# Memory attention of a streaming encoder step: prompt scores directly behind the second key product, sample parts in one three-bank result, query weights between key loads

## The chip, the cores and the metric

The kernel runs on one core of one Trainium2 chip. The metric is the device time of one execution in microseconds (us). PE is TensorE, DVE is VectorE, ACT is ScalarE, POOL is GpSimd; SP is the engine from whose queue most transfers are issued.

## The reference, cut to what matters

One layer with three parallel branches for 1024 prompt rows and 8 x 16 sample rows, then a merge and a ConvFFN. The change is in the third branch, cross-attention to 256 memory tokens with 4 heads of width 256. The prompt group computes its memory keys and values here; the sample group reads its own from a cache.

```python
def _mem_kv(mem, g, w):
    kv = (_rmsnorm(mem, g) @ w).reshape(B, M, 2, MEM_HEADS, MEM_DH)
    return (transpose(kv[:, :, 0], (0, 2, 1, 3)), transpose(kv[:, :, 1], (0, 2, 1, 3)))

def _mem_attention(q, mk, mv):
    q = q.reshape(B, L, MEM_HEADS, MEM_DH)
    logits = einsum('blhd,bhmd->bhlm', q, mk) * (MEM_DH ** -0.5)
    p = softmax(logits, axis=-1)
    return einsum('bhlm,bhmd->blhd', p, mv).reshape(B, L, MEM_HEADS * MEM_DH)
```

The prompt's keys and values per head (`new_mem_k_prompt`, `new_mem_v_prompt`) are outputs as well.

## The kernel before, in words

The program is a row of phases. `mem_phase` is the third branch. It runs its four heads one after the other: three in a hardware loop, the fourth written behind it (`head(MH - 1, last=True)`). The engines run apart and meet at semaphores. Each engine executes its own list in the order in which it is written.

**Results.** PE writes into two groups of four PSUM banks (512 float32 each), in turn. `Results` lists what a head writes, in order: K0, SL, K1, PTS, KR, S, V, OS, PT, OT, O0, O1, X, Y. `take` makes PE wait until the result two places back has been read (`free`); `ready` makes a reader wait until the result is whole (`full`); `freed` marks it as read.

One head on PE (`head` in the tensor block, lines 1741 to 1847):
- K0, K1 (`memory_keys`): the two halves of the head's memory keys, in split precision, 24 matmuls each. SL between them: the sample group's scores (L1765). ACT copies K0 and K1 to `mem_kt` (L1601). DVE and ACT make the softmax of SL (L1689, L1690, L1597, L1695 to L1697).
- PTS: four transposes of the sample probabilities (L1774); ACT copies them to `sample_probs_t` (L1604). KR: four transposes of the keys for the output (L1781); ACT copies them (L1607) and stores them (L1609).
- S: the prompt's scores, 16 products in two recorded passes (L1787). DVE takes the row maximum (L1689) and subtracts it (L1690), ACT takes the exponential (L1614), DVE sums (L1695), inverts (L1696) and scales (L1697). This last step releases PT.
- V: the memory values (L1800 to L1802). ACT copies them to `mem_v_rows` (L1616).
- OS: the sample's output (L1811), copied by ACT (L1623). PT: 16 transposes of the prompt's probabilities (L1818), copied by ACT (L1625). OT: four transposes of OS (L1824).
- O0, O1: the prompt's output (L1836). X, Y and "riders" in spare banks of OT, O0, O1: the next head's queries (L165 to L167), in six pieces. The first piece is in OT and needs the query weights W_Q[0]; the first that needs W_Q[1] is in X.

**Weights.** Blocks of 128 x 1024 go through two slots: SP loads one (`load_w`, L107) once POOL has finished the block before it in that slot, ACT rounds it to `weight_hi` (`round_w`, L113), POOL subtracts to get `weight_lo` (`rest_w`, L118), PE takes both (`w_parts`). A head uses six: W_K (2, from the head before), W_V (2), W_Q (2). In the fourth head, the W_Q slots take the next phase's branch weights.

**SP's order in a head** (`head`, lines 1537 to 1548): W_V[0], W_V[1]; the 32 loads of the next head's cached keys (`load_k`, L1530, eight streams with four loads each); W_Q[0], W_Q[1]; the next head's W_K; the eight loads of the next cached values (L1535). In the fourth head, there are no key or value loads. The cached keys are turned by DVE (L1679), streams 0 to 3 after PT, streams 4 to 7 after O1.

**ACT's order in a head**, behind K1: round W_V[1]; copy PTS; copy and store KR; exponential of S; copy V; round W_Q[0] and W_Q[1]; store the values; copy OS; copy PT.

Of the kernel before, what the change touches and what calls it, by code (L numbers as in the profile page):

```python
# [10 lines left out]
ACT = mybir.ActivationFunctionType  # L11
AX = mybir.AxisListType
ds = bass.ds

P = 128
D = 1024
KT = D // P
SEQ, DEC_B, DEC_S, PAST = 1024, 8, 16, 1024
ROWS = SEQ + DEC_B * DEC_S
NT = ROWS // P  # L20
PT = SEQ // P
# [3 lines left out]
MEM, MH, MD = 256, 4, 256  # L25
# [364 lines left out]
def flat(ap):  # L390
    return ap.rearrange("p a n -> p (a n)")
# [1075 lines left out]
def mem_phase(g):  # L1467
# [7 lines left out]
    MT = MEM // P  # L1475
    mq, yc = (g.sb(n, [P, 2, ROWS], ctx=ctx) for n in ("mem_q", "mem_out"))
    mk, mkr, mvr, ps_s, pt_s, qp = (g.sb(n, [P, 2, 256], ctx=ctx) for n in (
        "mem_kt", "mem_k_rows", "mem_v_rows", "sample_probs", "sample_probs_t", "mem_query_blocks"))
# [5 lines left out]
    gcol = g.sb("mem_norm_col", [P, KT], ctx=ctx)  # L1484
    rows, tmp = pr[:].rearrange("p (t a) n -> p t (a n)", t=MT), flat(pt[:]).rearrange("p (k n) -> p k n", k=KT)
    consts_in, cb = g.consts, g.cb
    kt_r = g.sem("cached_mem_k_turned")
    kc_in = [g.sem(f"cached_mem_k{n}_in") for n in range(2)]
    vc_in, sq_r, root_r, scaled, mhi_r, mlo_r, zero_r, qp_r = (g.sem(n) for n in (
        "cached_mem_v_in", "mem_squares", "mem_root", "mem_scaled",  # L1490
# [1 line left out]
    shift_r, probs_r, s_shift_r, s_probs_r, out_mk, out_mv, out_y = (g.sem(n) for n in (  # L1492
        "mem_shifted", "mem_probs_ready", "mem_sample_shifted", "mem_sample_probs_ready", "mem_k_out", "mem_v_out",
        "y2_out"))
    NW = 6
    first = 2
    W_K, W_V, W_Q = (first, first + 1), (first + 2, first + 3), (first + 4, first + 5)
    pre = Results(g, ["Q0", "N", "Q1"])
    g.r += pre.n
    loop_R = Results(g, ["K0", "SL", "K1", "PTS", "KR", "S", "V", "OS", "PT", "OT", "O0", "O1", "X", "Y"])  # L1500
    last_R = Results(g, [n for n in loop_R.k if n not in ("X", "Y")])
    last_R.base += (MH - 1) * loop_R.n
    assert loop_R.n % 2 == 0 and last_R.n % 2 == 0
# [6 lines left out]
    with nc.Block() as block:  # L1510
        @block.sync
        def _(sp):
            sp.dma_start(rows, g.x["mem_prompt"][0].rearrange("(t p) d -> p t d", p=P)).then_inc(consts_in, 16)
            with nc.allow_non_contiguous_dma(reason="columns of 1024 values"):
                sp.dma_start(gcol[:], columns(g.x["mem_norm"][0])).then_inc(consts_in, 16)

            def wkv(v, n, i):

                w = g.x["w_mem_kv"][0].rearrange("(k p) n -> p k n", p=P)
                return w[:, :, ds(i * MD + (v * D + n * P), P)]  # L1520

            def wq(n, i):
                return g.w_in(W_MQ + n, i, 2)

            def load_k(i):

                for b in range(DEC_B):
                    blocks = g.x["cache_mem_k"][0, b, ds(i, 1)].rearrange("h (r j) (c n) -> r (h j c) n", r=BLOCK, c=2)
                    for q in range(P // BLOCK):
                        sp.dma_start(kc[q * BLOCK:(q + 1) * BLOCK, b].rearrange("r c (j n) -> r (c j) n", n=BLOCK),  # L1530
                                     blocks[:, :, q * BLOCK:(q + 1) * BLOCK]).then_inc(kc_in[b // 4], 16)

            def load_v(i):
                for b in range(DEC_B):
                    sp.dma_start(vc[:, b], g.x["cache_mem_v"][0, b, ds(i, 1)].rearrange("h (t p) d -> p (h t) d", p=P))\  # L1535
                        .then_inc(vc_in, 16)

            def head(i, following, last=False):
                for n in range(2):
                    g.load_w(sp, wkv(1, n, i), W_V[n], i, NW)  # L1540
                if not last:
                    sp.wait_ge(kt_r, i * 2 + 2)
                    load_k(i + 1)
                for j, view in enumerate(following):
                    g.load_w(sp, view, W_Q[0] + j, i, NW)
                if not last:
                    sp.wait_ge(g.full, loop_R.full_value("OS", i))
                    load_v(i + 1)
            g.load_w(sp, wkv(0, 0, 0), W_K[0])
            g.load_w(sp, wkv(0, 1, 0), W_K[1])  # L1550
            load_k(0)
            load_v(0)
            with sp.Fori(0, MH - 1) as i:
                head(i, (wq(2, i), wq(3, i), wkv(0, 0, i + 1), wkv(0, 1, i + 1)))
            wb = g.x["w_branch"][0, 0].rearrange("(k p) n -> p k n", p=P)

            head(MH - 1, (wb[:, :, 0:P], wb[:, :, P:2 * P]), last=True)

        @block.scalar
        def _(act):  # L1560
            ps = pre.ready(act, "Q0")
# [10 lines left out]
            ps = pre.ready(act, "Q1")  # L1572
# [9 lines left out]
            def head(i, last=False):  # L1582
                R, r = (last_R, 0) if last else (loop_R, i)
# [4 lines left out]
                def finish(n, ins):  # L1588

                    if n in riders and not last:  # L1590
                        ins = query(*riders[n], g.psum[(R.base + R.k[n]) % 2], 3)
                    R.freed(ins, n)
                for n in range(2):
                    if n == 1:
                        ps = R.ready(act, "SL", r)
# [4 lines left out]
                    ps = R.ready(act, f"K{n}", r)  # L1600
                    finish(f"K{n}", act.activation(mk[:, n, :], ps[:, 0, 0:MEM], ACT.Copy))  # L1601
                    g.round_w(act, W_V[n], i, NW)
                ps = R.ready(act, "PTS", r)
                finish("PTS", act.activation(flat(pt_s[:]), ps[:, 0, :], ACT.Copy))  # L1604
                act.wait_ge(out_mk, i * 16 + 16)
                ps = R.ready(act, "KR", r)
                finish("KR", act.activation(mkr[:], ps[:, 0, :].rearrange("p (t n) -> p t n", t=MT), ACT.Copy))  # L1607
                R.wait_freed(act, "KR", r)
                act.dma_start(g.o["mk_prompt"][0, 0, ds(i, 1)].rearrange("h (t p) d -> p (h t) d", p=P), mkr[:])\  # L1609
                    .then_inc(out_mk, 16)  # L1610
                act.wait_ge(out_mv, i * 16 + 16)
                act.wait_ge(shift_r, i + 1)
                ps = R.ready(act, "S", r)
                finish("S", act.activation(flat(pr[:]), flat(ps), ACT.Exp))  # L1614
                ps = R.ready(act, "V", r)
                finish("V", act.activation(mvr[:], ps[:, 0, :].rearrange("p (t n) -> p t n", t=MT), ACT.Copy))  # L1616
                for n in range(2):
                    g.round_w(act, W_Q[n], i, NW)
                R.wait_freed(act, "V", r)
                act.dma_start(g.o["mv_prompt"][0, 0, ds(i, 1)].rearrange("h (t p) d -> p (h t) d", p=P), mvr[:])\  # L1620
                    .then_inc(out_mv, 16)
                ps = R.ready(act, "OS", r)
                finish("OS", act.activation(ps_s[:], ps[:, 0:2, 0:MD], ACT.Copy))  # L1623
                ps = R.ready(act, "PT", r)
                finish("PT", act.activation(flat(pt[:]), flat(ps), ACT.Copy))  # L1625
                act.wait_ge(out_y, i * 16 + 16)
                ps = R.ready(act, "OT", r)
# [3 lines left out]
                for c in range(2):  # L1631
                    ps = R.ready(act, f"O{c}", r)
# [3 lines left out]
                if not last:  # L1636
                    g.round_w(act, W_K[0] + NW, i, NW)
                    ps = R.ready(act, "X", r)
# [86 lines left out]
        def _(pe):  # L1725
# [15 lines left out]
            def head(i, last=False):  # L1741
# [5 lines left out]
                def take(n):  # L1747

                    ps = R.take(pe, n, r)
                    if n in riders and not last:  # L1750
                        return ps, query(ps, 3, *riders[n])
                    return ps, None
# [14 lines left out]
                                            start=(c == 0), stop=(c == 1))  # L1767
                ins.then_inc(g.full, 1)
                memory_keys(1)
                ps, _ = take("PTS")  # L1770
                pe.wait_ge(s_probs_r, i + 1)
                for n in range(2):
                    for m in range(MT):
                        ins = pe.transpose(ps[:, 0, (n * MT + m) * P:(n * MT + m + 1) * P],  # L1774
                                           ps_s[:, n, m * P:(m + 1) * P], g.ident[:])
                ins.then_inc(g.full, 1)
                ps, _ = take("KR")
                R.wait_freed(pe, "K1", r)
                for t in range(MT):
                    for n in range(2):  # L1780
                        ins = pe.transpose(ps[:, 0, t * MD + n * P:t * MD + (n + 1) * P], mk[:, n, t * P:(t + 1) * P],  # L1781
                                            g.ident[:])
                ins.then_inc(g.full, 1)
                ps, _ = take("S")
                for t in range(PT):
                    for n in range(2):
                        ins = pe.matmul(ps[:, t // 2, (t % 2) * MEM:(t % 2 + 1) * MEM], mq[:, n, t * P:(t + 1) * P],  # L1787
# [1 line left out]
                ins.then_inc(g.full, 1)  # L1789

                ps, _ = take("V")
                for n in range(2):
                    g.w_parts(pe, W_V[n], i, NW)
                wh, wl = (t[:].rearrange("p n (k c) -> p k n c", c=P) for t in (g.whi, g.wlo))
                if (g.w + W_V[0]) % 2:
                    raise ValueError("the first value block stands in the first slot")
                for t in range(MT):
                    rows_t, o = slice(t * P, (t + 1) * P), ps[:, 0, t * MD:(t + 1) * MD].rearrange("p (n c) -> p n c", c=P)
                    for k in range(KT):
                        pe.matmul(o, mhi[:, k, rows_t], wh[:, k], start=(k == 0), stop=False)  # L1800
                        pe.matmul(o, mlo[:, k, rows_t], wh[:, k], start=False, stop=False)
                        ins = pe.matmul(o, mhi[:, k, rows_t], wl[:, k], start=False, stop=(k == KT - 1))  # L1802
                ins.then_inc(g.full, 1)
                ps, _ = take("OS")
                R.wait_freed(pe, "PTS", r)
                pe.wait_ge(vc_in, i * 128 + 128)
                pv = flat(pt_s[:]).rearrange("p (n m q) -> p n m q", n=2, m=MT)
                for n in range(2):
# [870 lines left out]
```

## Time and profile before

| what | us |
|---|---|
| median of 3 runs | 3334.06 (3327.71 to 3336.87) |
| profiled execution, its own time | 3333.16 |
| its span in the profile | 3331.4 |
| PE busy, whole span | 3145.9 (94%) |
| DVE, ACT, POOL busy | 1388.3, 1127.7, 874.1 |
| the four heads, K0 of the first to the merge's first matmul | 1726.85 to 2004.63 |

A row of the timeline gives the start and the duration in us, the engine, the line, what is written and read, a count, and in brackets how long the engine was idle before it and what released it. A row of waits gives who waited for whom: total, times, longest. Where two rows of one engine overlap, that is its pipeline.

### The profile page before, as it was taken

To read this page: it belongs to the slowest core of one execution; us is meant where nothing else is said; L and a number is where in the kernel's file an instruction comes from. 1 tells how busy PE (TensorE), PEld (TensorE's weight loads), DVE (VectorE), ACT (ScalarE), POOL (GpSimd) and SP (SyncE) were. 2 spreads that over 40 slices of the span, in tenths; PEclk is the share of its full clock that TensorE was granted. 3 is DMA by queue.
4 is the path that set the end of the run, shared out by engine and by line. 5 is a ranking of instruction groups with operands and counts; after the bars stand their busy time and mean duration, and the time that the engine had idled before them with its cause. 6 is when DMAs were issued, how large, how long until landed. Compare 5 with 4: busy or idle time off the path is not lost. (4 is left out here: it accounts for less than half of the span.)

```text
span 3331.4 us, 50040 instructions
## 1 busy us (share of the span) xinstructions
PE 3145.9 (94%) x19550; PEld 2959.6 (89%) x19550; DVE 1388.3 (42%) x1446; ACT 1127.7 (34%) x1586; POOL 874.1 (26%) x520
## 2 busy tenths in 40 slices
PE   6999999999999999999679889999979999999997
PEld 5999999999988888888467769999979999999996
DVE  5554444544344555455522212222044444444433
ACT  3344433444234444444432221122242222222222
POOL 2433233332211121121011211343342322322220
PEclk8999999999999999999789899999989999999998
DMA  5212121112157787678665526432211111111101
GB/s 158 72 46 66 56 69 55 50 60 63 57 112 152 153 138 121 139 147 142 120 144 127 134 91 208 148 105 67 79 51 45 44 38 44 39 42 38 38 25 68
DMA packets 684752, 295.69 MB, mean 89 GB/s; under 512 B 350524, under 2 KB 665436, under 8 KB 684680
## 3 DMA queue, kind: packets, MB, share of 16 engines
q1 hardware_dynamic: 680232, 285.90, 35.2%
q10 hardware_dynamic: 4448, 8.80, 0.7%
q8 instruction: 49, 0.80, 0.1%
q14 instruction: 23, 0.19, 0.0%
HBM read 240.23 MB, written 54.41 MB: 88 GB/s over the span
## 5 line engine op out<-in xcount | busy, mean ns | idle before, releaser
L118 POOL TENSOR_TENSOR weight_lo<-weight_stage,weight_hi 128x1024 fp32r<-128x1024 f32 x180 | 452.4, 2515 | 1483.3 <-ACT weight_hi L113 1483.3
L1862 PE MATMUL group<-act_hi_part,weight_hi 128*128 128x384 f32 x1056 | 360.8, 342 | 13.6 <-DVE act_lo_part L2091 9.3
L1863 PE MATMUL group<-act_lo_part,weight_hi 128*128 128x384 f32 x1056 | 359.8, 341 | 0.0
L1864 PE MATMUL group<-act_hi_part,weight_lo 128*128 128x384 f32 x1056 | 359.7, 341 | 0.0
L165 PE MATMUL group<-h_hi_part,weight_hi 128*128 128x384 f32 x936 | 331.5, 354 | 9.9 <-POOL weight_lo L118 4.8
L113 ACT ACTIVATE weight_hi<-weight_stage 128x1024 fp32r<-128x1024 f32 x180 | 190.7, 1061 | 419.8 <-PE group L2133 231.6
L166 PE MATMUL group<-h_lo_part,weight_hi 128*128 128x384 f32 x936 | 317.2, 339 | 0.0
L167 PE MATMUL group<-h_hi_part,weight_lo 128*128 128x384 f32 x936 | 317.0, 339 | 0.0
L2131 PE MATMUL group<-act_hi_part,weight_hi 128*128 128x384 f32 x768 | 259.5, 338 | 11.9 <-DVE act_lo_part L2044 11.9
L2132 PE MATMUL group<-act_lo_part,weight_hi 128*128 128x384 f32 x768 | 258.6, 337 | 0.0
L2133 PE MATMUL group<-act_hi_part,weight_lo 128*128 128x384 f32 x768 | 258.6, 337 | 0.0
L1350 PE MATMUL group<-h_hi_part,weight_hi 128*128 128x384 f32 x696 | 243.8, 350 | 1.1 <-ACT next_v L1096 1.0
L1350 PE MATMUL group<-h_hi_part,weight_lo 128*128 128x384 f32 x696 | 237.8, 342 | 0.0
L1350 PE MATMUL group<-h_lo_part,weight_hi 128*128 128x384 f32 x696 | 235.6, 339 | 0.0
L1862 PEld LDWEIGHTS group<-act_hi_part,weight_hi 128*128 128x128 f32 x1056 | 199.6, 189 | 17.1 <-issue 9.9
L698 DVE COPY_PREDICATED scores<-level_masks,group 128x1152 f32<-128x1152 uint32 (+2 forms) x88 | 92.2, 1078 | 285.1 <-PE group L823 283.9
L1863 PEld LDWEIGHTS group<-act_lo_part,weight_hi 128*128 128x128 f32 x1056 | 199.7, 189 | 0.0
L1864 PEld LDWEIGHTS group<-act_hi_part,weight_lo 128*128 128x128 f32 x1056 | 199.6, 189 | 0.0
L165 PEld LDWEIGHTS group<-h_hi_part,weight_hi 128*128 128x128 f32 x936 | 178.5, 191 | 16.5 <-POOL weight_lo L118 5.1
L166 PEld LDWEIGHTS group<-h_lo_part,weight_hi 128*128 128x128 f32 x936 | 178.3, 191 | 4.3 <-issue 3.3
L167 PEld LDWEIGHTS group<-h_hi_part,weight_lo 128*128 128x128 f32 x936 | 177.9, 190 | 0.0
L2408 DVE TENSOR_TENSOR residual<-residual,group 128x1152 f32<-128x1152 f32 x80 | 108.3, 1354 | 163.3 <-PE group L2523 163.3
(348 smaller groups left out, 6694.3 us busy)
## 6 DMA issues: line engine op xcount, KB each, us to landing
weight_stage<-in_w_in SPq DMA_DIRECT2D x88, 512.0 KB, 4.8
cached_v<-in_cache_diff_v SPq DMA_DIRECT2D x128, 256.0 KB, 5.0
cached_k<-in_cache_diff_k SPq DMA_DIRECT2D x224, 128.0 KB, 4.2
weight_stage<-in_w_up SPq DMA_DIRECT2D x44, 512.0 KB, 3.8
y_stage<-scratch_y_branch SPq DMA_DIRECT2D x24, 576.0 KB, 9.4
gate_in<-scratch_gates SPq DMA_DIRECT2D x24, 576.0 KB, 3.7
weight_stage<-in_w_branch SPq DMA_DIRECT2D x24, 512.0 KB, 3.9
down_stage<-in_w_down SPq DMA_DIRECT2D x22, 512.0 KB, 3.6
```

The costliest lines, as they stand in the source:

```text
L113: act.activation(self.whi[:, n % 2, :], self.wst[:, n % 2, :], ACT.Copy).then_inc(self.w_hi, 1)
L118: pool.tensor_tensor(self.wlo[:, n % 2, :], self.wst[:, n % 2, :], self.whi[:, n % 2, :].bitcast(F32), ALU.subtract).then_inc(self.w_lo, 1)
L165: pe.matmul(out, wh[:, k, :], xh[:, k, cols], start=(k == 0), stop=False)
L166: pe.matmul(out, wh[:, k, :], xl[:, k, cols], start=False, stop=False)
L167: last = pe.matmul(out, wl[:, k, :], xh[:, k, cols], start=False, stop=(k == KT - 1))
L1350: ins = pe.matmul(rider_bank, w[:, k, :], x[:, k, c * CW:(c + 1) * CW], start=(at == 0), stop=(at == STEPS - 1))
L1862: pe.matmul(o, w[0][:, k, :], ahi[:, k, rows], start=(k == 0), stop=False)
L1863: pe.matmul(o, w[0][:, k, :], alo[:, k, rows], start=False, stop=False)
L1864: last = pe.matmul(o, w[1][:, k, :], ahi[:, k, rows], start=False, stop=(k == KT - 1))
L2131: pe.matmul(o, wh[:, k, :], ahi[:, k, cols], start=(k == 0 and open_sum), stop=False)
L2132: pe.matmul(o, wh[:, k, :], alo[:, k, cols], start=False, stop=False)
L2133: last = pe.matmul(o, wl[:, k, :], ahi[:, k, cols], start=False, stop=(k == KT - 1))
```

## The change

Three things, all in `mem_phase`.

1. PE computes S directly behind K1. The transposes of sample probabilities and keys go behind it.
2. PTS and KR are no results of their own any more. Both are written into banks 0 and 1 of V's group, the values into bank 2. A head has 12 results instead of 14. ACT reads the three in a row once V is whole: sample probabilities, keys, values. A new semaphore, `turned_r`, tells PE that the sample probabilities are copied; OS waits for it. The key store is issued beside the value store.
3. SP issues W_Q[0] behind the key loads of streams 0 to 2, and W_Q[1] behind those of stream 3, instead of both behind all eight. ACT rounds W_Q[1] behind the copy of OS instead of ahead of it.

```diff
-    loop_R = Results(g, ["K0", "SL", "K1", "PTS", "KR", "S", "V", "OS", "PT", "OT", "O0", "O1", "X", "Y"])
+    loop_R = Results(g, ["K0", "SL", "K1", "S", "V", "OS", "PT", "OT", "O0", "O1", "X", "Y"])
...
-                    load_k(i + 1)
-                for j, view in enumerate(following):
-                    g.load_w(sp, view, W_Q[0] + j, i, NW)
+                    load_k(i + 1, range(0, 3))
+                g.load_w(sp, following[0], W_Q[0], i, NW)
+                if not last:
+                    load_k(i + 1, range(3, 4))
+                g.load_w(sp, following[1], W_Q[1], i, NW)
+                if not last:
+                    load_k(i + 1, range(4, DEC_B))
+                for j, view in enumerate(following[2:]):
+                    g.load_w(sp, view, W_Q[1] + 1 + j, i, NW)
...
-                ps = R.ready(act, "PTS", r)
-                finish("PTS", act.activation(flat(pt_s[:]), ps[:, 0, :], ACT.Copy))
-                act.wait_ge(out_mk, i * 16 + 16)
-                ps = R.ready(act, "KR", r)
-                finish("KR", act.activation(mkr[:], ps[:, 0, :].rearrange("p (t n) -> p t n", t=MT), ACT.Copy))
-                R.wait_freed(act, "KR", r)
-                act.dma_start(g.o["mk_prompt"][0, 0, ds(i, 1)].rearrange("h (t p) d -> p (h t) d", p=P), mkr[:])\
-                    .then_inc(out_mk, 16)
-                act.wait_ge(out_mv, i * 16 + 16)
                 act.wait_ge(shift_r, i + 1)
                 ps = R.ready(act, "S", r)
                 finish("S", act.activation(flat(pr[:]), flat(ps), ACT.Exp))
                 ps = R.ready(act, "V", r)
-                finish("V", act.activation(mvr[:], ps[:, 0, :].rearrange("p (t n) -> p t n", t=MT), ACT.Copy))
-                for n in range(2):
-                    g.round_w(act, W_Q[n], i, NW)
+                act.activation(flat(pt_s[:]), ps[:, 0, :], ACT.Copy).then_inc(turned_r, 1)
+                act.wait_ge(out_mk, i * 16 + 16)
+                act.wait_ge(out_mv, i * 16 + 16)
+                act.activation(mkr[:], ps[:, 1, :].rearrange("p (t n) -> p t n", t=MT), ACT.Copy)
+                finish("V", act.activation(mvr[:], ps[:, 2, :].rearrange("p (t n) -> p t n", t=MT), ACT.Copy))
+                g.round_w(act, W_Q[0], i, NW)
                 R.wait_freed(act, "V", r)
+                act.dma_start(g.o["mk_prompt"][0, 0, ds(i, 1)].rearrange("h (t p) d -> p (h t) d", p=P), mkr[:])\
+                    .then_inc(out_mk, 16)
...
                 finish("OS", act.activation(ps_s[:], ps[:, 0:2, 0:MD], ACT.Copy))
+                g.round_w(act, W_Q[1], i, NW)
...
-                R.wait_freed(pe, "PTS", r)
+                pe.wait_ge(turned_r, i + 1)
```

On PE, the place is the head from the last matmul of K1 (L152) to the first of V. Before:

```order
L152 MATMUL group<-mem_hi_part,weight_lo 128x256
L370 REGISTER_ALU
L1774 MATMUL group<-ident,sample_probs 128x128 x4
L1781 MATMUL group<-ident,mem_kt 128x128 x4
L370 REGISTER_ALU
L1787 MATMUL group<-mem_kt,mem_q 128x256 x16
L123 REGISTER_ALU x2
L1800 MATMUL group<-weight_hi,mem_hi_part 128x256
```

And with the change, where the same instructions stand on other lines (L1777 is the scores, L1785 and L1789 the transposes):

```order
L152 MATMUL group<-mem_hi_part,weight_lo 128x256
L370 REGISTER_ALU
L1777 MATMUL group<-mem_kt,mem_q 128x256 x16
L1785 MATMUL group<-ident,sample_probs 128x128 x4
L1789 MATMUL group<-ident,mem_kt 128x128 x4
L123 REGISTER_ALU x2
L1799 MATMUL group<-weight_hi,mem_hi_part 128x256
```

The eight transposes went from ahead of the scores to behind them.

On ACT, the place is the fourth head from the copy of K1 to the copy of PT (in the loop the order is the same). Before:

```order
L1601 ACTIVATE mem_kt<-group 128x256
L113 ACTIVATE weight_hi<-weight_stage 128x1024
L1604 ACTIVATE sample_probs_t<-group 128x512
L1607 ACTIVATE mem_k_rows<-group 128x512
L1609 DMA out_mk_prompt<-mem_k_rows 128x2x256
L1614 ACTIVATE mem_probs<-group 128x2048
L1616 ACTIVATE mem_v_rows<-group 128x512
L113 ACTIVATE weight_hi<-weight_stage 128x1024 x2
L1620 DMA out_mv_prompt<-mem_v_rows 128x2x256
L1623 ACTIVATE sample_probs<-group 128x512
L1625 ACTIVATE mem_probs_t<-group 128x2048
```

And with the change:

```order
L1607 ACTIVATE mem_kt<-group 128x256
L113 ACTIVATE weight_hi<-weight_stage 128x1024
L1611 ACTIVATE mem_probs<-group 128x2048
L1613 ACTIVATE sample_probs_t<-group 128x512
L1616 ACTIVATE mem_k_rows<-group 128x512
L1617 ACTIVATE mem_v_rows<-group 128x512
L113 ACTIVATE weight_hi<-weight_stage 128x1024
L1620 DMA out_mk_prompt<-mem_k_rows 128x2x256
L1622 DMA out_mv_prompt<-mem_v_rows 128x2x256
L1625 ACTIVATE sample_probs<-group 128x512
L113 ACTIVATE weight_hi<-weight_stage 128x1024
L1628 ACTIVATE mem_probs_t<-group 128x2048
```

Two copies went behind the exponential, and one rounding went behind the copy of OS.

On SP, the place is the loop's end of the key loads before the change:

```order
L1530 DMA cached_mem_k<-in_cache_mem_k 32x16x32
L106 REGISTER_ALU
L107 ISA
L107 DMA weight_stage<-in_w_in 128x8x128
L106 REGISTER_ALU
L107 ISA
L107 DMA weight_stage<-in_w_in 128x8x128
L106 REGISTER_ALU
L107 ISA
L107 DMA weight_stage<-in_w_mem_kv 128x8x128
```

And with the change, behind the twelfth of the 32 key loads:

```order
L1530 DMA cached_mem_k<-in_cache_mem_k 32x16x32
L106 REGISTER_ALU
L107 ISA
L107 DMA weight_stage<-in_w_in 128x8x128
L1530 ISA
L1530 DMA cached_mem_k<-in_cache_mem_k 32x16x32
```

The first query block now passes 20 key loads, the second 16.

## Rows read from the trace of the kernel before

**Rows 1.** The page, busy us (share of the span) xinstructions of each engine.

```profile
PE 3145.9 (94%) x19550; PEld 2959.6 (89%) x19550; DVE 1388.3 (42%) x1446; ACT 1127.7 (34%) x1586; POOL 874.1 (26%) x520
```

**Rows 2.** Waits, 1720 to 2000 us: who <- for whom: total, times, longest.

```profile
PE group L1818 <- DVE mem_probs L1697: 13.1, 4, 4.2
...
PE group L1824 <- ACT sample_probs L1623: 8.1, 2, 4.6
```

**Rows 3.** Timeline of head 1 on PE, K1's end to OT.

```profile
1813.76 0.63 PE L1774 MATMUL group<-ident,sample_probs 128*128 128x128 f32 x4 [1.49 <-DVE sample_probs L1697]
1814.23 0.60 PE L1781 MATMUL group<-ident,mem_kt 128*128 128x128 f32 x4
1815.08 7.17 PE L1787 MATMUL group<-mem_kt,mem_q 128*128 128x256 f32 x32 [0.25 <-ACT sample_probs_t L1604]
...
1829.09 1.93 PE L1811 MATMUL group<-cached_mem_v,sample_probs_t 128*32 128x256 f32 x32 [1.09 <-ACT mem_probs L1614]
1833.99 3.46 PE L1818 MATMUL group<-ident,mem_probs 128*128 128x128 f32 x16 [2.97 <-DVE mem_probs L1697]
1840.95 1.09 PE L1824 MATMUL group<-ident,sample_probs 128*128 128x128 f32 x4 [3.50 <-ACT sample_probs L1623]
```

**Rows 4.** Timeline of head 1 on DVE, POOL and ACT.

```profile
1831.55 2.29 DVE L1697 TENSOR_TENSOR mem_probs<-mem_probs,mem_row_sum 128x2048 f32<-128x2048 f32 x1
...
1808.85 2.39 POOL L118 TENSOR_TENSOR weight_lo<-weight_stage,weight_hi 128x1024 fp32r<-128x1024 f32 x1 [0.35 <-ACT weight_hi L113]
...
1812.31 0.38 ACT L1601 ACTIVATE mem_kt<-group 128x256 f32<-128x256 f32 x1 [0.34 <-PE group L152]
...
1827.08 1.88 ACT L1614 ACTIVATE mem_probs<-group 128x2048 f32<-128x2048 f32 x1 [11.57 <-DVE group L1690]
1828.85 0.59 ACT L1616 ACTIVATE mem_v_rows<-group 128x512 f32<-128x512 f32 x1
1837.60 1.06 ACT L113 ACTIVATE weight_hi<-weight_stage 128x1024 fp32r<-128x1024 f32 x1 [8.16 <-DMA weight_stage<-in_w_in]
```

**Rows 5.** Timeline of SP's queue in head 1: issues, and the time they took SP.

```profile
1809.33 23.91 SPq L1530 DMA_DIRECT2D cached_mem_k<-in_cache_mem_k  x32
1833.49 1.03 SPq L107 DMA_DIRECT2D weight_stage<-in_w_in  x2
```

**Rows 6.** Heads 0, 2, 3 on PE and ACT: K1's copy, scores, V's last matmul, OT.

```profile
1743.64 0.42 ACT L1601 ACTIVATE mem_kt<-group 128x256 f32<-128x256 f32 x1
...
1747.76 9.15 PE L1787 MATMUL group<-mem_kt,mem_q 128*128 128x256 f32 x32
...
1885.35 7.17 PE L1787 MATMUL group<-mem_kt,mem_q 128*128 128x256 f32 x32 [0.25 <-ACT sample_probs_t L1604]
...
1897.99 0.28 PE L1802 MATMUL group<-weight_lo,mem_hi_part 128*128 128x256 f32 x1
...
1911.44 1.08 PE L1824 MATMUL group<-ident,sample_probs 128*128 128x128 f32 x4 [4.62 <-ACT sample_probs L1623]
...
1953.62 0.38 ACT L1601 ACTIVATE mem_kt<-group 128x256 f32<-128x256 f32 x1 [0.29 <-PE group L152]
...
1956.70 8.80 PE L1787 MATMUL group<-mem_kt,mem_q 128*128 128x256 f32 x32 [0.51 <-ACT sample_probs_t L1604]
```

**Rows 7.** Timeline of head 3 on POOL and DVE: weight rests beside the scaling.

```profile
1973.62 6.71 POOL L118 TENSOR_TENSOR weight_lo<-weight_stage,weight_hi 128x1024 fp32r<-128x1024 f32 x2 [15.05 <-ACT weight_hi L113]
...
1974.71 3.42 DVE L1697 TENSOR_TENSOR mem_probs<-mem_probs,mem_row_sum 128x2048 f32<-128x2048 f32 x1
```

**Rows 8.** Windows, head 2: us, PE, PEld, DVE, ACT, POOL busy (x), PEclk, DMA share, GB/s.

```profile
1904.20:1911.40 7.20, 2.56 (x16) 2.19 (x16) 2.31 (x1) 2.70 (x4) 2.10 (x1) 0.58 0.66 182
```

**Rows 9.** Timeline of PE, head 2: query matmuls behind OT.

```profile
1912.18 0.67 PE L165 MATMUL group<-h_hi_part,weight_hi 128*128 128x384 f32 x1
...
1915.94 0.34 PE L165 MATMUL group<-h_hi_part,weight_hi 128*128 128x384 f32 x1
1916.11 0.34 PE L166 MATMUL group<-h_lo_part,weight_hi 128*128 128x384 f32 x1
```

More of the change, by code:

```diff
@@ L1486, in mem_phase @@
     consts_in, cb = g.consts, g.cb
-    kt_r = g.sem("cached_mem_k_turned")
+    kt_r, turned_r = g.sem("cached_mem_k_turned"), g.sem("sample_probs_turned")
     kc_in = [g.sem(f"cached_mem_k{n}_in") for n in range(2)]
@@ L1523, in wq, with load_k @@
                 return g.w_in(W_MQ + n, i, 2)
-            def load_k(i):
-                for b in range(DEC_B):
+            def load_k(i, streams):
+                for b in streams:
                     blocks = g.x["cache_mem_k"][0, b, ds(i, 1)].rearrange("h (r j) (c n) -> r (h j c) n", r=BLOCK, c=2)
@@ L1550, in _ @@
             g.load_w(sp, wkv(0, 1, 0), W_K[1])
-            load_k(0)
+            load_k(0, range(DEC_B))
             load_v(0)
@@ L1769, in head @@
                 memory_keys(1)
[L1770 to L1777, printed above, removed]
-                R.wait_freed(pe, "K1", r)
[L1779 to L1784, printed above, removed]
+                ps, _ = take("S")
+                R.wait_freed(pe, "K1", r)
                 for t in range(PT):
@@ L1791, in head @@
                 ps, _ = take("V")
+                pe.wait_ge(s_probs_r, i + 1)
+                for n in range(2):
+                    for m in range(MT):
+                        pe.transpose(ps[:, 0, (n * MT + m) * P:(n * MT + m + 1) * P],
+                                           ps_s[:, n, m * P:(m + 1) * P], g.ident[:])
+                for t in range(MT):
+                    for n in range(2):
+                        pe.transpose(ps[:, 1, t * MD + n * P:t * MD + (n + 1) * P], mk[:, n, t * P:(t + 1) * P],
+                                            g.ident[:])
                 for n in range(2):
@@ L1797, in head @@
                 for t in range(MT):
-                    rows_t, o = slice(t * P, (t + 1) * P), ps[:, 0, t * MD:(t + 1) * MD].rearrange("p (n c) -> p n c", c=P)
+                    rows_t, o = slice(t * P, (t + 1) * P), ps[:, 2, t * MD:(t + 1) * MD].rearrange("p (n c) -> p n c", c=P)
                     for k in range(KT):
```

## The prediction

> **What bounds the kernel now.** I read the page first: PE is busy for 94% of the span [rows 1], so little can be won outside PE's gaps. Then the waits in the stretch of the memory heads: PE stands 13.1 us before PT (L1818) for DVE's scaling, in all four heads, and 8.1 us before OT (L1824) for ACT's copy of OS, in two [rows 2]. Then the timeline of head 1. The reader is to see two chains.
>
> The first begins at the scores S: they start at 1815.08, and PT, which needs their softmax, at 1833.99 [rows 3]. These 18.91 us are S on PE, two passes of DVE, the exponential on ACT (from 1827.08), the sum, the inverse and the scaling on DVE (1831.55 + 2.29 = 1833.84) [rows 4]. PE's own work between (V, OS) is shorter: it stands 1.09 and 2.97 us [rows 3]. So PT moves with the start of S, us for us, as long as V and OS still fit in. S itself waits for what stands ahead of it: the sample transposes, which wait 1.49 us for the sample softmax [rows 3].
>
> The second is the weights. ACT can't copy OS before it has rounded both query blocks, and it stands 8.16 us for the first, until 1837.60 [rows 4]. The block was late at its issue: SP issued 32 key loads from 1809.33 for 23.91 us and the query blocks only at 1833.49 [rows 5]. OT starts at 1840.95 after 3.50 us of idle PE [rows 3], in head 2 after 4.62 [rows 6]; and the waits name no third head [rows 2].
>
> The heads are a serial chain on PE, and the phases behind them too, so what is won in a head should stay won.
>
> **The change, part by part.**
>
> *S directly behind K1.* S now waits for ACT's copy of K1 alone. In head 1 that ends at 1812.31 + 0.38 = 1812.69 [rows 4]; with 0.1 for the semaphore S starts at 1812.8 instead of 1815.08: **2.3 us**. Head 2 repeats head 1: **2.3**. In head 0 the copy ends at 1744.06, S started at 1747.76: **3.6**. In head 3 it ends at 1954.00, S started at 1956.70: **2.6** [rows 6]. The chain from S to PT is unchanged, so PT comes earlier by the same.
>
> *Do the moved parts still fit?* Counted from the start of S: V's last matmul ended at 1897.99 + 0.28 - 1885.35 = 12.9 us [rows 6]. The eight transposes now stand ahead of V; four took 0.47 from start to start [rows 3], so eight add 0.95, and V is whole at 13.9. The exponential ends at 1827.08 + 1.88 - 1815.08 = 13.9 too. Then ACT copies the sample probabilities, and OS can start at about 14.6, instead of 14.0; it takes 1.93 [rows 3] and ends at 16.6. PT starts at 18.9. So OS is later and PE still waits there, 2.3 us: nothing is lost. Two results less cost nothing, their waits went with them. The key store's issue goes from before the exponential to beside the value store; both stand ahead of the copy of OS on ACT's queue. That copy isn't late until PT has ended, 21.5 at the earliest, against 16.6 + 0.6: cover of 4 us.
>
> *Query weights earlier.* A key load costs SP 23.91 / 32 = 0.75 us. W_Q[0] goes out behind 12 of them, at 1809.33 + 9.0 = 1818.3 (its slot is free: the rest of W_V[0] was done at 1808.85 + 2.39 = 1811.24 [rows 4]). Before, it was rounded 1837.60 - 1833.49 = 4.1 us behind its issue; now it lands at some 1822.5, and ACT wants it only at 1828.2. If the loads around it doubled its time it were still in time. W_Q[1] follows at 1821.8, lands at 1826, is wanted at 1830. Key loads of streams 3 to 7 come 0.5 to 1 us later, DVE turns stream 3 behind PT, 10 us after its landing, and the others behind O1: covered. So the wait before OT goes: **3.5 us** in head 1, **4.6** in head 2. What is late next there is PT itself, whose end releases OT.
>
> *The scaling and POOL.* In head 3 the scaling (L1697) took 3.42 us instead of 2.29, while POOL worked on weight rests that had started 1.09 before it; the two rests took 6.71, against 2.39 for one elsewhere [rows 4, 7]. One reading fits both to the tenth: POOL's first rest ran alone until about 1975.9, then DVE's 2.29 until 1978.13, then the second rest until 1980.3. That is no slower work, but one waiting for the whole of the other. The Trainium skill ("SBUF — State Buffer", section "Who interferes with whom") says so: a DVE instruction with two SBUF inputs and a GpSimd instruction that reads SBUF exclude each other, and whichever issues first holds the port for its whole length. By that rule the trace agrees, and the rule speaks against this change.
>
> For the change moves a rest to exactly this place in all four heads. From S's start: pt_s copied from 13.9, keys and values at intervals of 0.48 (a copy's busy 0.59, overlapped), W_Q[0] rounded from 15.4 to 16.4 (1.06 us [rows 4]), POOL at 16.5. The scaling starts at 1831.55 - 1815.08 = 16.47. That is a tie within what these numbers can tell. Bounds: if DVE is first, 0, and head 3 gets back its 3.42 - 2.29 = **1.1 us**; if POOL is first, the scaling waits up to 2.4, PT comes 2.3 us later in each head. I take DVE first: each of my shortcuts (a switch between kinds of matmul, ACT's additional waits for the stores) makes POOL later, none makes DVE later.
>
> *PE's clock.* After the long wait for OT the granted clock was down: 0.58 over the stretch from PT to OT in head 2 [rows 8], that is in good part the lower level, 1.2 of 2.4 GHz. The query matmuls then went 12 in 3.76 us, where 12 take 2.1 at 0.17 [rows 9]: 1.7 lost. Head 3's scores took 8.80 instead of 7.17 [rows 3, 6]: 1.6 lost after the gaps around the transposes, and these gaps go. Bounds: 0, and 1.7 + 1.6 with at most another 1.7 in head 1 = 5.0. PE still has gaps before OS and PT, and PT may lose in head 2 what the query wins, so I take **2**.
>
> *Sum.* 3.6 + (2.3 + 3.5) + (2.3 + 4.6) + (2.6 + 1.1) = 20.0, and 2 for the clock: 22 us. The profiled execution took 3333.16 of its own time, 0.9 under the median of the runs. 3333.16 - 22 = **3311 us**.
>
> **Rivals.**
>
> *POOL gets the port first.* Then the scaling waits 2.3 us in each head, and the gain of S directly behind K1 is used up: 4 x 2.3 = 9.3 less. 3311 + 9 = 3320. For it: the tie; a mere 0.1 us decides. Against it: it needs V to be whole no later than 13.9 in every head. By the skill's rule and this order it would be this time.
>
> *PE's clock recovers everywhere, in head 0's scores (9.15 against 7.17) as well.* Upper bound 5.0 + 2.0 instead of 2: 3306. For it: shorter gaps in all heads; against it: PE stands some 3 us before head 0's scores as before.
>
> *The query blocks come late from between the key loads (slower).* Place: ACT's rounding of W_Q[1], which now stands ahead of the copy of PT. If the small loads around it hold it up, the copy, O0, O1 and all behind wait. Before, the copy of PT began behind OT's start at 1840.9; for a head to lose, W_Q[1] must land after 1839.9 (1.06 us of rounding ahead of that), 18 us behind its issue at 1821.8, instead of 4.1. At 25 us the copy of PT would begin 7 us later than before in three heads, and head 3 would keep its gain: 3333 + 21 - 4 = 3350. Against it: measured landings; nothing in the trace comes near.
>
> *The change does not take effect:* S isn't earlier because K1's copy is itself held up on ACT by a weight (in head 0 it stood behind one). Only the weights' gain stays, 8.1 + 1.1: 3324.
>
> **How the numbers follow.** About 0.3%, 10 us, is what a measurement of this kernel can tell from no change; the runs shown lie within 9 us. Chances: the forecast 0.55, POOL first (in most heads) 0.30, full clock 0.08, no effect 0.04, late blocks 0.03. The range goes from 3303 (full clock, and a few us of spread between runs) to 3323 (POOL first with no clock won back: 3322). Under 3324 is faster: the forecast, the full clock, and most of POOL first: 0.88. Within 10 us: the rest of it and no effect: 0.10. Slower: 0.02.
>
> **What would show it.** In the trace after: in heads 1 and 2 S within 0.2 us behind K1's copy; no idle before OT; PT 18.9 us behind the start of S at full clock. If the scaling takes 4 to 4.7 us with a POOL rest started just before it, POOL was first. If it takes 2.29 and POOL's rest 4 to 4.7, DVE was. If ACT stands before a rounding of W_Q for a load, the place between the key loads is too late. I am wrong if PT doesn't move with S, or if the heads get shorter and the phases behind them longer.

## The result and the profile after

The changed kernel takes 3297.26 us (median of 4 runs, 3292.19 to 3301.82) against 3332.64 for the kernel before on the same chip (4 runs): ratio 0.9896, 95% interval 0.9883 to 0.9909. That is 35 us faster, 30 to 39 by the interval. I had forecast 3311 with a range of 3303 to 3323: the direction was right, the gain was half as large again, and the range misses it. The profiled execution is the longest of the four, 3301.82; it is 31.3 us under the profile before, and it misses the range too. What follows explains these 31.3; no profile was taken of a run near 3292, so some 4 us of the median's gain stay without a place.

First the page of the changed kernel; the line answers to [rows 1].

```profile
PE 3131.9 (95%) x19550; PEld 2949.7 (89%) x19550; DVE 1387.6 (42%) x1446; ACT 1128.4 (34%) x1586; POOL 881.0 (27%) x520
```

PE has the same 19550 matmuls and is busy for 14 us less. So it isn't only waits that went. To see where, I cut both traces at the same events: K0 of head 0, the end of the copy of K1 in each head, the merge's first matmul. Windows of the kernel before (us, PE, PEld, DVE, ACT, POOL busy, PEclk, DMA share, GB/s), first the stretch ahead of the heads, the heads together, and the stretch behind them; then heads 0 to 3, each from its copy of K1 to the next:

```profile
0.00:1726.85 1726.85, 1633.55 (x10809) 1489.54 (x10809) 841.40 (x1079) 707.95 (x1066) 421.29 (x224) 0.98 0.46 100
1726.85:2004.63 277.78, 225.84 (x1377) 192.20 (x1377) 70.31 (x50) 77.56 (x97) 56.79 (x23) 0.90 0.48 128
2004.63:3331.40 1326.77, 1286.56 (x7366) 1277.87 (x7366) 476.64 (x319) 342.23 (x424) 396.03 (x274) 0.98 0.21 66
...
1744.06:1812.69 68.63, 62.23 (x380) 54.24 (x380) 17.78 (x13) 20.61 (x26) 15.89 (x7) 0.93 0.51 131
1812.69:1882.96 70.27, 60.97 (x380) 53.50 (x380) 16.93 (x12) 20.41 (x27) 14.19 (x6) 0.95 0.51 129
1882.96:1954.00 71.04, 60.62 (x380) 52.98 (x380) 16.88 (x13) 19.13 (x26) 14.19 (x6) 0.93 0.49 126
1954.00:2004.63 50.63, 30.80 (x157) 22.63 (x157) 12.76 (x10) 13.29 (x14) 9.05 (x3) 0.80 0.26 90
```

And of the changed kernel:

```profile
0.00:1726.55 1726.55, 1632.37 (x10808) 1489.23 (x10809) 841.74 (x1079) 708.62 (x1066) 421.83 (x224) 0.97 0.46 100
1726.55:1973.03 246.48, 212.76 (x1376) 182.35 (x1377) 69.31 (x50) 77.50 (x97) 63.05 (x23) 0.96 0.55 144
1973.03:3300.00 1326.97, 1286.80 (x7366) 1278.11 (x7366) 476.57 (x319) 342.30 (x424) 396.11 (x274) 0.98 0.21 66
...
1743.66:1808.34 64.68, 60.99 (x380) 53.41 (x380) 17.80 (x13) 20.43 (x27) 17.92 (x7) 0.95 0.55 139
1808.34:1869.70 61.36, 57.67 (x380) 50.60 (x380) 16.93 (x13) 20.44 (x27) 16.38 (x6) 1.00 0.59 148
1869.70:1931.05 61.35, 57.67 (x380) 50.60 (x380) 16.87 (x13) 19.14 (x26) 16.37 (x6) 1.00 0.58 146
1931.05:1973.03 41.98, 25.19 (x156) 19.00 (x157) 11.76 (x10) 13.53 (x15) 9.07 (x3) 0.92 0.31 110
```

Ahead of and behind the heads nothing changed. The heads lost 31.3 us (277.78 to 246.48). PE's idle time there, stretch less busy, fell from 51.94 to 33.72: **18.2 us**. Its busy time for the same matmuls fell by **13.1 us**, and the granted clock rose from 0.90 to 0.96, in heads 1 and 2 to 1.00. By heads 0 to 3, idle fell by 2.7, 5.6, 6.7 and 3.0, busy by 1.2, 3.3, 3.0 and 5.6.

The timeline of head 1 on PE in the changed kernel, to be laid beside [rows 3]:

```profile
1808.49 7.14 PE L1777 MATMUL group<-mem_kt,mem_q 128*128 128x256 f32 x32 [0.56 <-ACT mem_kt L1607]
1823.13 1.93 PE L1810 MATMUL group<-cached_mem_v,sample_probs_t 128*32 128x256 f32 x32 [0.87 <-ACT sample_probs_t L1613]
1827.32 1.94 PE L1817 MATMUL group<-ident,mem_probs 128*128 128x128 f32 x16 [2.25 <-DVE mem_probs L1700]
```

S starts 0.15 us behind the copy of K1 (1807.96 + 0.38), PT 18.83 behind S, and there is no gap before OT. PT takes 1.94 where it took 3.46. The groups by line and form in the heads give the sums over all four: S, O and PT, first of the kernel before and then of the changed one (busy, mean ns | idle before).

```profile
L1787 PE MATMUL group<-mem_kt,mem_q 128*128 128x256 f32 x128 | 32.3, 416 | 1.0 <-ACT sample_probs_t L1604 1.0
L1836 PE MATMUL group<-mem_probs_t,mem_v_rows 128*128 128x512 f32 x64 | 30.3, 621 | 1.2 <-ACT mem_probs_t L1625 1.2
L1818 PE MATMUL group<-ident,mem_probs 128*128 128x128 f32 x64 | 13.1, 392 | 13.1 <-DVE mem_probs L1697 13.1
```

```profile
L1777 PE MATMUL group<-mem_kt,mem_q 128*128 128x256 f32 x128 | 30.3, 397 | 4.9 <-ACT mem_kt L1607 4.9
L1835 PE MATMUL group<-mem_probs_t,mem_v_rows 128*128 128x512 f32 x64 | 28.7, 593 | 1.6 <-ACT mem_probs_t L1628 1.6
L1817 PE MATMUL group<-ident,mem_probs 128*128 128x128 f32 x64 | 9.1, 304 | 9.0 <-DVE mem_probs L1700 9.0
```

In head 0 PT still went slowly, behind the same gap as in the other heads:

```profile
1764.33 3.29 PE L1817 MATMUL group<-ident,mem_probs 128*128 128x128 f32 x16 [2.23 <-DVE mem_probs L1700]
```

The other engines in head 1: DVE's scaling, POOL's two rests and ACT's rounding of W_Q[0].

```profile
1824.89 2.29 DVE L1700 TENSOR_TENSOR mem_probs<-mem_probs,mem_row_sum 128x2048 f32<-128x2048 f32 x1
...
1824.90 6.86 POOL L118 TENSOR_TENSOR weight_lo<-weight_stage,weight_hi 128x1024 fp32r<-128x1024 f32 x2 [12.68 <-ACT weight_hi L113]
...
1823.75 1.07 ACT L113 ACTIVATE weight_hi<-weight_stage 128x1024 fp32r<-128x1024 f32 x1
```

The scaling took 2.29, the two rests 6.86; in heads 0 to 2 of the kernel before they took 4.67 to 4.73:

```profile
1838.74 4.67 POOL L118 TENSOR_TENSOR weight_lo<-weight_stage,weight_hi 128x1024 fp32r<-128x1024 f32 x2 [22.18 <-ACT weight_hi L113]
```

DVE was first, by 0.01 us as recorded, and by 0.01 to 0.09 in the other heads. ACT didn't wait for W_Q[0]: no idle is recorded before the rounding.

### The profile page after: what moved, and what is told of

Same layout as the page of the kernel before. It is cut to its first block and busy times, and to the rows that moved or that the text cites. A ratio compares the mean times of both kernels' runs of the same rounds, so it can differ in the third digit from the quotient of the medians.

```text
span 3300.0 us, 50028 instructions
## 1 busy us (share of the span) xinstructions
PE 3131.9 (95%) x19550; PEld 2949.7 (89%) x19550; DVE 1387.6 (42%) x1446; ACT 1128.4 (34%) x1586; POOL 881.0 (27%) x520
## 5 line engine op out<-in xcount | busy, mean ns | idle before, releaser
L118 POOL TENSOR_TENSOR weight_lo<-weight_stage,weight_hi 128x1024 fp32r<-128x1024 f32 x180 | 459.6, 2554 | 1447.1 <-ACT weight_hi L113 1447.0
```

The lines of the kernel that those rows point to most:

```text
L118: pool.tensor_tensor(self.wlo[:, n % 2, :], self.wst[:, n % 2, :], self.whi[:, n % 2, :].bitcast(F32), ALU.subtract).then_inc(self.w_lo, 1)
```

## The experiments

Two theories for the 9 us beyond the forecast's 22: **the clock** (PE's shorter gaps keep the granted clock up, and the same matmuls take less time) and **the waits** (more waits went than I counted). A third question is what each part is worth alone, a fourth the port. The heads' stretch below runs from K0 of head 0 to the merge's first matmul, as above.

**Scores first, weights where they were.** SP's order of the kernel before in the changed kernel. ACT still rounds W_Q[1] behind the copy of OS, so this is the first two parts and ACT's half of the third:

```diff
-                    load_k(i + 1, range(0, 3))
-                g.load_w(sp, following[0], W_Q[0], i, NW)
...
+                    load_k(i + 1, range(DEC_B))
+                for j, view in enumerate(following):
+                    g.load_w(sp, view, W_Q[0] + j, i, NW)
```

> The change without its third part: scores behind K1 and the three-bank result stay, the query weights go out behind all 32 key loads again. Theory (two separate waits, and the clock follows the gaps): in heads 1 and 2 PT starts 2.3 us earlier, but OT still waits for the copy of OS behind the late W_Q[0], and only 1.6 us are won there; head 0 wins 2.2, head 3 (no key loads) its whole 8.6. Sum 14, about 0.4%: some 3319 against 3333. Rival (all of the extra gain comes from the merged results and fewer waits on PE, not from gaps and clock): heads 1 and 2 keep most of their 9 us, 3305 or less.

3325.43 against 3332.61, ratio 0.9979 (0.9968 to 0.999); the stretch 274.01, 3.8 less than before. The sign was right and the size wrong. OT now waits in all three heads of the loop (total idle at the right):

```profile
L1817 PE MATMUL group<-ident,sample_probs 128*128 128x128 f32 x16 | 3.9, 389 | 16.7 <-ACT sample_probs L1619 16.7
...
1837.61 1.09 PE L1817 MATMUL group<-ident,sample_probs 128*128 128x128 f32 x4 [6.04 <-ACT sample_probs L1619]
1839.19 0.69 PE L165 MATMUL group<-h_hi_part,weight_hi 128*128 128x384 f32 x1 [0.49 <-POOL weight_lo L118]
```

What S wins, OT waits longer, for the weights arrive when they did. I had counted 2.2 for head 0, where OT did not wait before: it now waits 4.29. Behind the longer gap the query runs slow for longer: in head 1 about 5.6 us where it was about 2.3. Heads 0 to 2 got longer by 3.6, 1.1 and 0.6 us, head 3 shorter by 8.7. So the first two parts pay in head 3 alone, which has no key loads.

**Weights alone.** The third part on the kernel before (SP as in the diff of the change; on ACT):

```diff
-                for n in range(2):
-                    g.round_w(act, W_Q[n], i, NW)
+                g.round_w(act, W_Q[0], i, NW)
...
                 finish("OS", act.activation(ps_s[:], ps[:, 0:2, 0:MD], ACT.Copy))
+                g.round_w(act, W_Q[1], i, NW)
```

> Only the third part on the kernel before: W_Q[0] behind 12 key loads, W_Q[1] behind 16, ACT rounds W_Q[1] behind the copy of OS. Theory with the port (whichever of DVE's scaling and POOL's rest starts first holds the other off for its whole length): without the three copies ACT rounds W_Q[0] one us earlier, POOL starts 15.4 us behind the scores' start, ahead of the scaling at 16.5; the scaling takes some 3.5 us instead of 2.29 in all four heads and PT is 1.2 later. OT's waits of 3.5 and 4.6 us go, the clock gives 1 to 2: sum 5 to 7, some 3327. Rival (no exclusion, the rows of head 3 were something else): scaling 2.29, sum 9 to 11, 3323.

3322.92, ratio 0.9963 (0.9949 to 0.9977); the stretch 270.71, 7.1 less. The median is the rival's 3323, the 7.1 stands at the upper end of the theory's 5 to 7, so the times do not decide; the rows do. The groups of the scaling and of PT:

```profile
L1703 DVE TENSOR_TENSOR mem_probs<-mem_probs,mem_row_sum 128x2048 f32<-128x2048 f32 x4 | 13.7, 3418 | 0.1
...
L1824 PE MATMUL group<-ident,mem_probs 128*128 128x128 f32 x64 | 14.4, 419 | 16.4 <-DVE mem_probs L1703 16.4
```

The scaling takes 3.42 in all four heads: POOL is first everywhere, as the theory with the port says. PE's gap before PT grew to 4.1, and PT went at the lower clock in all heads (14.4 us against 9.1 in the changed kernel).

So these two kernels give 3.8 and 7.1 us of the stretch, and the whole change 31.3. Each alone runs into a wait that the other part removes or shortens.

**PT delayed.** One more pass on DVE in the changed kernel:

```diff
-                    dve.tensor_tensor(p, p, sm[:, 0:blocks].unsqueeze(2).to_broadcast([P, blocks, MEM]), ALU.mult)\
-                        .then_inc(ready, 1)
+                    ins = dve.tensor_tensor(p, p, sm[:, 0:blocks].unsqueeze(2).to_broadcast([P, blocks, MEM]), ALU.mult)
+                    if blocks == PT:
+                        g.dve.done(ins)
+                        ins = dve.tensor_reduce(sm[:, 0:blocks], p, AX.X, ALU.add)
+                    ins.then_inc(ready, 1)
```

> The change with one more DVE pass (a sum over the scaled probabilities, 2.3 us) between the scaling and its signal to PE, so PE's gap before PT is 4.6 us instead of 2.25 in all four heads. Theory (the extra gain over the forecast is PE's clock, which stays up while the gaps are short): 4 x 2.4 = 9.6 us of delay and besides the transposes of PT at half clock (1.94 becomes 3.5) and the matmuls behind them slow for a while, 2.5 to 4 per head: 18 to 24 us slower than the change, some 3318. Rival (waits alone): 9.6 slower, 3307, with PT still taking 1.94.

3313.69, ratio 0.9939 (0.9922 to 0.9955). The stretch, and PT's group:

```profile
1723.90:1985.22 261.32, 218.08 (x1376) 187.64 (x1377) 78.36 (x53) 77.29 (x97) 62.98 (x23) 0.93 0.52 136
...
L1820 PE MATMUL group<-ident,mem_probs 128*128 128x128 f32 x64 | 13.9, 409 | 18.4 <-DVE mem_row_sum L1703 18.4
```

14.8 more than the changed kernel: idle 43.2 instead of 33.7, which is the delay (18.4 - 9.0 = 9.4 before PT), and 5.3 more of busy PE for the same matmuls. The waits' 9.6 are too few, and my 18 to 24 too many: PT fell to the lower clock in all heads (4.8 of the 5.3), the matmuls behind it hardly did.

**Gaps filled.** Matmuls nobody reads, in the kernel before; no wait is touched:

```diff
+                def fill(o, n):
+                    for k in range(n):
+                        pe.matmul(o, mhi[:, k % KT, 0:P], mhi[:, k % KT, :], start=True, stop=True)
...
+                fill(ps[:, 0, 0:MEM], 18)
                 pe.wait_ge(probs_r, i + 1)
...
+                fill(g.psum[(R.base + R.k["OS"]) % 2][:, 3, 0:MEM], 16)
                 ps = R.take(pe, "OT", r)
```

> The kernel before, with matmuls on the memory parts whose results nobody reads: 18 (2.1 us) in the gap before PT and 16 (1.9 us) behind PT, ahead of OT's wait. No wait is shortened. Theory (clock): PT takes 1.94 instead of 2.56 to 3.65 in all heads, the queries behind OT run at full clock in heads 1 and 2, the products O of head 3 too: 9 to 10 won, 1.9 lost in head 0 where OT has no gap: 7 to 8 us faster than before, 3325. Rival (clock doesn't matter): 0 to 4 us slower than before.

3328.44, ratio 0.9982 (0.9972 to 0.9992): 136 more matmuls make the kernel 3 to 9 us faster (the heads 4.2 shorter in the profile). PT of head 1, and its group:

```profile
1835.94 1.97 PE L1824 MATMUL group<-ident,mem_probs 128*128 128x128 f32 x16 [0.54 <-DVE mem_probs L1697]
...
L1824 PE MATMUL group<-ident,mem_probs 128*128 128x128 f32 x64 | 9.3, 308 | 3.4 <-DVE mem_probs L1697 3.4
```

PT took 1.97 in heads 0 to 2 and still 3.44 in head 3; this, a longer gap ahead of the sample transposes in head 0 (5.81 us against 5.06) and the scores of head 2 (8.86 us against 7.17) kept the gain under the 7 to 8 expected. PT still starts 18.83 us behind S in head 1 (18.91 before), so no wait got shorter. That the time of equal matmuls falls when PE's gaps are filled, with every wait in place, is shown for PT in heads 0 to 2.

**The changed kernel again**, beside the next three on another chip.

> The changed kernel again, on the same chip as the three below. Theory: the stretch of the heads takes 246 to 247 us as before, with 212 to 213 us of busy PE in it; if the time differs from the first profile's 3302, the difference lies in other phases. Rival (the heads themselves come out differently from run to run, by the clock): the stretch differs by over 3 us.

3301.05 against 3331.8, ratio 0.9903 (0.9886 to 0.992). Its stretch:

```profile
1727.46:1974.25 246.79, 212.42 (x1376) 182.15 (x1377) 69.19 (x49) 76.79 (x96) 62.95 (x23) 0.96 0.55 143
```

The heads repeat to 0.3 us; the 3.0 us between the two profiles lie ahead of them (0.9) and behind them (1.8). But where PE goes slowly does not repeat: here head 0's PT took 1.94, and head 2's, which took 1.94 in the first profile, went slowly behind the same gap:

```profile
1888.53 3.52 PE L1817 MATMUL group<-ident,mem_probs 128*128 128x128 f32 x16 [2.25 <-DVE mem_probs L1700]
```

**No common result.** Scores first and the weights' new places, but PTS and KR stay results of their own, behind S:

```diff
-"K1", "PTS", "KR", "S", "V", "OS"
+"K1", "S", "PTS", "KR", "V", "OS"
```

> Scores directly behind K1 and the weights' new places, but the sample transposes and the key transposes stay results of their own, each in the whole group, behind the scores (K1, S, PTS, KR, V). Theory (two groups in turn: KR must wait until the exponential has read S, 13.9 us behind the start of S): V starts at 14.6 instead of 7.8, OS ends at 22.7, PT starts at 22.8 instead of 18.9: 3.9 us per head and PE's clock low in V behind a gap of 6: 16 to 26 us slower than the change, 3313 to 3323. Rival (merging the three only saves a few semaphore waits): within 4 us of the change.

3322.05, ratio 0.9965 (0.9952 to 0.9977). KR in head 1, and the stretch:

```profile
1825.18 1.11 PE L1793 MATMUL group<-ident,mem_kt 128*128 128x128 f32 x4 [6.27 <-ACT mem_probs L1611]
...
1725.34:1990.96 265.62, 218.40 (x1376) 187.16 (x1377) 69.30 (x50) 77.55 (x96) 54.52 (x23) 0.91 0.51 134
```

18.8 us more than the change. KR waits 6.27 for the exponential, since it needs S's group, and V with it. Against the weights alone (270.71) the new place of S brings only 5.1 us of the stretch here: most of its worth hangs on the three banks.

**The port.** W_Q[0] rounded ahead of the copies of keys and values:

```diff
                 act.activation(flat(pt_s[:]), ps[:, 0, :], ACT.Copy).then_inc(turned_r, 1)
+                g.round_w(act, W_Q[0], i, NW)
...
-                g.round_w(act, W_Q[0], i, NW)
```

> The change with one thing moved on ACT: W_Q[0] is rounded directly behind the copy of the sample probabilities, ahead of the copies of keys and values, so that POOL's rest starts one us earlier, 15.5 us behind the start of S instead of 16.5. Theory (the port goes to whichever starts first, for its whole length): the scaling's 2.29 becomes 3.4 to 3.7 in all four heads, PT comes 1.2 later, its gap grows to 3.4 and its clock falls in some heads: 5 to 11 us slower than the change. Rival (no exclusion, or no tie): scaling 2.29, no difference over 2 us, since nothing else waits for those copies.

3313.22, ratio 0.9947 (0.993 to 0.9964): 12 us more than the change on the same chip by the medians. Head 1, and the stretch:

```profile
1825.98 3.55 DVE L1700 TENSOR_TENSOR mem_probs<-mem_probs,mem_row_sum 128x2048 f32<-128x2048 f32 x1
...
1825.02 2.36 POOL L118 TENSOR_TENSOR weight_lo<-weight_stage,weight_hi 128x1024 fp32r<-128x1024 f32 x1 [11.66 <-ACT weight_hi L113]
...
1829.68 1.94 PE L1817 MATMUL group<-ident,mem_probs 128*128 128x128 f32 x16 [3.51 <-DVE mem_probs L1700]
...
1724.63:1981.98 257.35, 217.99 (x1377) 186.91 (x1377) 74.30 (x49) 77.24 (x97) 57.16 (x23) 0.93 0.53 138
```

POOL's rest ends at 1827.38; the scaling, issued at 1825.98, ends 2.15 us after that: it waited for nearly all of what was left of the rest, as "Who interferes with whom" in "SBUF — State Buffer" of the Trainium skill says. That is 1.26 us in heads 1 and 2 (1.25 and 1.34 in the others), and 10.6 in the stretch: 5.0 of idle, 5.6 of busy PE. In head 1 PT took 1.94 all the same; in the other heads it took 2.75 to 3.65.

**Softmax in halves.** DVE's work on the first four row blocks runs while PE makes the other four:

```diff
+                    if t == PT // 2 - 1:
+                        ins.then_inc(half_r, 1)
...
+                for h in range(2):
+                    if h == 0:
+                        dve.wait_ge(half_r, i + 1)
+                    else:
+                        R.ready(dve, "S", r)
+                    v, m = s[:, h * H:(h + 1) * H], mx[:, h * H:(h + 1) * H]
+                    g.dve.done(dve.tensor_reduce(m, v, AX.X, ALU.max))
+                    dve.tensor_tensor(v, v, m.unsqueeze(2).to_broadcast([P, H, MEM]), ALU.subtract).then_inc(shift_r, 1)
```

> The change with the prompt softmax in two halves of four row blocks: DVE's maximum and subtraction of the first half run while PE still makes the second, the exponential and the scaling go by halves, PT by halves. Theory (PE's gap before PT is the chain S, DVE, ACT, DVE): the scaling ends at some 15.5 us behind the start of S instead of 18.8, PT follows OS with no gap: 4 x 2.25 = 9 us less idle, 1 to 2 of clock in head 0: 9 to 11 us faster than the change, ratio to before 0.986. Rival (the rest of POOL, now without the scaling beside it, or the copy of OS becomes what OT waits for): 4 us or less.

3290.38, ratio 0.9869 (0.9852 to 0.9885), where the change on the same chip had 0.9903. The stretch, and the scaling of head 1 as two instructions:

```profile
1725.08:1963.22 238.14, 212.49 (x1376) 181.64 (x1377) 70.77 (x61) 77.52 (x100) 54.39 (x23) 0.95 0.58 149
...
1818.46 2.36 DVE L1722 TENSOR_TENSOR mem_probs<-mem_probs,mem_row_sum 128x1024 f32<-128x1024 f32 x2
```

8.7 us less than the change, all of it idle (25.7 against 34.4); the busy time is the same, so the 1 to 2 us of clock that I expected did not come: head 0's scores took 9.93 us where they took 8.53. S started at 1805.06, so the scaling ends 15.8 behind it, and PT has no gap. This kernel beats the changed one, by 10.7 us by the medians.

## Why the prediction was wrong, step by step

- *S directly behind K1* and *the parts still fit*: right. In head 1, 18.83 from S to PT where I had 18.91, OS at 14.64 behind S where I had 14.6, PE's gap before PT 2.25 where I had 2.3.
- *Query weights earlier*: right, with no gap before OT and no wait for W_Q on ACT. The rival of late blocks did not happen.
- *The scaling and POOL*: right, and as close as I said. That DVE was first rests on 0.01 to 0.09 us, which my sums could not tell; that part was luck. The reading of head 3 before fits to 0.2 us, not to the tenth: the second rest, from 1978.13 to 1980.33, is 2.20 long, not 2.39. The rival's price was off: POOL one us earlier cost about 1.3 of wait per head, not 2.3, but as much again by the clock.
- The sum of waits, 20.0, measured 18.2. Heads 1 and 2 gave 5.6 and 6.7 of idle where I had 5.8 and 6.9. Heads 0 and 3 gave 2.7 and 3.0 where I had 3.6 and 3.7: in head 0 some 0.9 of the interval that I counted ahead of S was the lower clock in PE's transposes (the eight took 1.77 us there and 0.87 in the changed kernel), which counts as busy time; in head 3 PE now stands 0.5 longer behind OT (before O 1.62 instead of 1.21).
- **PE's clock is the step that failed**: "Bounds: 0, and 1.7 + 1.6 with at most another 1.7 in head 1 = 5.0", of which I took 2. It measured 13.1. The table gives PE's busy time by place, from windows of both traces:

| place | before | after | less | priced |
|---|---|---|---|---|
| OT and the queries up to O0, heads 1 and 2 | 20.94 | 17.58 | 3.4 | 3.4 |
| K1's copy to PT, head 3 (with the scores) | 17.54 | 15.71 | 1.8 | 1.6 |
| PT up to OT, four heads | 12.71 | 8.39 | 4.3 | no |
| OT to the merge, head 3 (with O) | 9.83 | 7.71 | 2.1 | no |
| K1's copy to OS, head 0 (with the scores) | 16.68 | 15.45 | 1.2 | by the rival alone |

Two of these places as windows, first of the kernel before and then of the changed one: OT and the queries of head 2, PT of head 3.

```profile
1911.44:1922.18 10.74, 10.74 (x52) 10.74 (x53) 0.00 (x0) 2.39 (x3) 2.54 (x2) 0.80 0.84 257
1978.27:1981.71 3.44, 3.44 (x16) 3.44 (x17) 0.00 (x0) 0.00 (x0) 2.07 (x1) 0.50 0.00 0
...
1890.45:1899.24 8.79, 8.79 (x54) 8.79 (x53) 2.31 (x1) 2.65 (x3) 2.66 (x2) 1.00 0.87 217
1949.96:1951.73 1.77, 1.77 (x16) 1.77 (x17) 0.00 (x0) 0.00 (x0) 1.77 (x1) 1.00 0.04 9
```

The five places hold 12.9 of the 13.1. The places that I priced gave the whole of the 5.0, and I had taken 2 of it. The rest is what I left out, PT above all: I even wrote that it might lose in head 2. The upper bound was none. That the granted clock stood at 0.90 over all four heads was to be read from a window before; it would have shown that more went slowly than the places that I priced. With the two measured terms, 18.2 and 13.1, 3333.16 becomes 3301.9, and the profiled execution took 3301.82.

- The rival of full clock priced the same term (3306): it took the 5.0 and added 2.0 for head 0's scores, and left out PT and O as well.

The waits' theory falls: idle fell by less than forecast, the busy time made up the rest, and in both runs that changed PE's gaps alone the time of the same matmuls moved with them (PT's 9.1 to 13.9 with the delay, 13.1 to 9.3 with the gaps filled). Open stays where the runs' spread, 3292 to 3302, comes from, and with it the 4 us of the median's gain: no phase outside the heads was studied. Open is also why of two equal gaps one is followed by the lower clock and one is not.

## What to carry to other kernels

A gap on PE can have two prices: itself, and the matmuls behind it at the lower clock; read the second as busy time of equal work, in a window over the whole stretch, not from the places that strike the eye. Two waits that hide each other must go together: the two halves of this change gave 3.8 and 7.1 us of the heads, the whole 31.3. Before moving work beside a DVE instruction with two SBUF inputs, look up where POOL's next instruction falls: here one us decided over 10.

## What the runs showed of the hardware that was not expected

The same 1376 matmuls took PE between 212.4 and 225.8 us of busy time, on the whole the more the longer PE stood idle among them: 212.4 to 212.8 beside 26 to 34 us of idle, 222.3 and 225.8 beside 52. The sum of idle time is not all: beside 47.2 us of it stood 218.4 (own results) and 223.5 (weights alone).

The length of one gap does not settle the clock behind it. Sixteen transposes behind a gap of 2.23 to 2.31 us took 1.94 in nine of twelve heads (the change, its repeat, the scores first) and 3.24 to 3.52 in three; behind 2.96 and 2.97 they took 2.56 to 3.46; behind 3.5 to 3.7 (W_Q[0] rounded early) 1.94 in one head and 2.75 to 3.65 in three; behind 4.1 to 4.6 3.37 to 3.65 in all nine. Matmuls without a use, put into the gaps, made the kernel before 3 to 9 us faster.
